# Merged delta-rule and attention stage: another order of the steps of neighbouring chunks, and five attention units in the lead-in

## The reference

```python
# DeltaNet, per chunk: A from keys and decays, a triangular solve, then the state recurrence
m = einsum(kb, kc) * decay;  a = tril(m, -1) + eye
u, w = solve(a, [v * beta, kb * exp(gcum)])
v_new = u - w @ S
o = (q * exp(g)) @ S + (q @ k.T * decay) @ v_new
S = S * exp(g_last) + (k * exp(g_last - g)).T @ v_new
# differential attention, per head and block of 128 queries, causal
amap = softmax(q1 k1) - lam * softmax(q2 k2);  out = amap @ v
```

## Time and profile before

| | |
|---|---|
| median of three runs | 1760.65 us |
| profiled execution | 1762.61 us |
| its span, first to last instruction | 1761.0 us |
| TensorE busy | 1644.0 us |
| VectorE busy | 996.0 us |
| ScalarE busy | 524.2 us |
| GpSimd busy | 290.5 us |
| merged stage | 434.8 to 730.4 us of the span |

### The profile page before, as it was taken

How to read it: one execution, slowest core, us unless ns; L and a number is a source line. 1 busy time by engine, 2 the same in 40 slices (tenths; PEclk the granted TensorE clock), 3 DMA queues, 4 the chain that set the end, 5 groups by cost and what they waited for, 6 DMA issues and landing times.

```text
span 1761.0 us, 27513 instructions
## 1 busy us (share of the span) xinstructions
PE 1644.0 (93%) x10506; PEld 1534.7 (87%) x10506; DVE 996.0 (57%) x1416; ACT 524.2 (30%) x810; POOL 290.5 (16%) x668
## 2 busy tenths in 40 slices
PE   5999999998789899788599999999999999999998
PEld 4999999897577787664399999999999999999997
DVE  4454368776467667337335565565564565555554
ACT  4344332332244344232322231122121221221214
POOL 2200012122555464233100000000000000000000
PEclk9999999999799999888699999999999999999999
DMA  4321111231112311272431221010210110111103
GB/s 143 123 60 39 45 40 37 74 98 61 51 34 55 85 27 35 72 273 72 154 84 39 73 60 59 25 60 16 67 58 14 60 60 24 60 48 36 48 0 108
DMA packets 144530, 113.34 MB, mean 64 GB/s; under 512 B 18987, under 2 KB 132157, under 8 KB 143030
## 3 DMA queue, kind: packets, MB, share of 16 engines
q1 hardware_dynamic: 138802, 100.43, 19.1%
q0 software_dynamic: 2304, 8.39, 1.3%
q10 hardware_dynamic: 3350, 3.53, 0.6%
HBM read 90.59 MB, written 21.74 MB: 64 GB/s over the span
## 4 chain that ended last, share of the span: by engine, by line
PE 48%; DVE 1%; ACT 1%; issue 0%; DMA 0%; SPq 0%; ACTq 0%; DVEq 0%
PE f_up L2905 28%; PE f_down L2912 14%; PE f_up L181 4%; PE f_up L2865 1%; PE f_up L2892 0%; PE f_up L2912 0%; PE f_up L2950 0%; DVE h_rstd L2745 0%; DMA f_rows<-in_ffn_conv_b 0%; DVE o_lo L2725 0%; PE f_up L2939 0%; PE f_down L2855 0%; ACT f_tail_tok L2673 0%; DVE w_lo L2694 0%; DVE dn_lo L2836 0%
## 5 line engine op out<-in xcount | busy, mean ns | idle before, releaser
L2905 PE MATMUL f_up<-h_hi,w_hi 128*128 128x352 f32 x1032 | 335.1, 325 | 1.9 <-DVE w_lo L2694 1.2
L2905 PE MATMUL f_up<-h_hi,w_lo 128*128 128x352 f32 x1032 | 333.4, 323 | 0.0
L2905 PE MATMUL f_up<-h_lo,w_hi 128*128 128x352 f32 x1032 | 333.4, 323 | 0.0
L181 PE MATMUL proj<-x_hi,win_hi 128*128 128x352 f32 x672 | 227.4, 338 | 5.3 <-issue 3.0
L181 PE MATMUL proj<-x_hi,win_lo 128*128 128x352 f32 x672 | 217.5, 324 | 0.0
L181 PE MATMUL proj<-x_lo,win_hi 128*128 128x352 f32 x672 | 217.3, 323 | 0.0
L2905 PEld LDWEIGHTS f_up<-h_hi,w_hi 128*128 128x128 f32 x1032 | 193.8, 188 | 2.5 <-DVE w_lo L2694 1.5
L2905 PEld LDWEIGHTS f_up<-h_hi,w_lo 128*128 128x128 f32 x1032 | 194.0, 188 | 0.0
L2905 PEld LDWEIGHTS f_up<-h_lo,w_hi 128*128 128x128 f32 x1032 | 193.8, 188 | 0.0
L2912 PE MATMUL f_down<-f_g_hi,dn_hi 128*128 128x352 f32 x512 | 165.3, 323 | 0.0
L2912 PE MATMUL f_down<-f_g_hi,dn_lo 128*128 128x352 f32 x512 | 164.7, 322 | 0.0
(11 more groups left out here) (438 smaller groups left out, 2932.4 us busy)
## 6 DMA issues: line engine op xcount, KB each, us to landing
w_raw<-in_w_up SPq DMA_DIRECT2D x44, 512.0 KB, 3.8
win_raw<-in_w_in SPq DMA_DIRECT2D x28, 512.0 KB, 4.1
dn_raw<-in_w_down SPq DMA_DIRECT2D x11, 1024.0 KB, 5.1
p_key<-in_cache_k SPq DMA_DIRECT2D x32, 256.0 KB, 3.5
feat<-in_cache_v POOLq DMA_DIRECT2D x24, 256.0 KB, 5.0
x_scratch<-feat SPq DMA_DIRECT2D x1, 4224.0 KB, 13.4
feat<-x_scratch SPq DMA_DIRECT2D x8, 528.0 KB, 8.8
feat<-in_x_prompt SPq DMA_DIRECT2D x8, 512.0 KB, 8.6
```

Source lines behind the costliest of these rows:

```text
L181: mm = nc.tensor.matmul(out, w[:, k, :], x[:, k, g * TG:(g + 1) * TG], start=(k == 0 and i == 0), stop=(k == KT - 1 and i == 2))
L2905: mm = nc.tensor.matmul(up[u % RING][:, 0:TG], a[s][:, kk, :], b, start=(kk + x == 0), stop=(kk == KT - 1 and x == 2))
```

## The change

The lead-in gets five periods with a unit each (EARLY = 5), so the plan has 37 periods. 27 units are left for the chunks; the last period of the chunks 3 to 7 has none, and chunk 7 has units in its first three. The key products and their weighting of chunk n + 2 (KK, B, so AT(n+2)) move to the last period of chunk n; KQ(n+1) goes to period 1, turn_keys(n+1) stays in period 2 but ahead of the scores, R(n+2) moves from period 3 to 2, V(n+1) stays in 3. state_w and state_next stand both in period 0, state_out in period 1, before the scores. `STEP` says in which lead-in period a step of chunk 0 or 1 stands. GpSimd does block_inverse before the first two cut_offs. The waits on the `side` bank follow the new order. The rest of the kernel is the same.

```diff
@@ -1053,14 +1053,24 @@
     v_rows = o["v_prompt"].rearrange("a b (n p) h d -> p (a b n) h d", p=P)
 
 
-    EARLY = 3
+    EARLY = 5
     plan, a = [], 0
     for n in range(-1, NC):
-        for p in range(PER):
-            free = n < 0 and p >= EARLY or n == NC - 1 and a >= NU
-            plan.append((n, p, None if free else a, plan[-1][2] if plan else None))
-            a += not free
-    assert a == NU and plan[-1][2] is None
+        for p in range(EARLY if n < 0 else PER):
+            left = NU - a
+            idle = n >= 0 and p == PER - 1 and left <= (PER - 1) * (NC - 1 - n)
+            plan.append((n, p, None if idle else a, plan[-1][2] if plan else None))
+            a += not idle
+    assert a == NU
+
+    STEP = {"keys_keys": (0, 3), "spread_beta": (0, 3), "cumulate": (None, 1), "keys_queries": (1, None), "turn_keys": (2, None),
+            "spread_decay": (None, 2), "turn_values": (3, None)}
+
+    def chunk_at(n, p, what, period, ahead):
+
+        if n < 0:
+            return STEP[what].index(p) if p in STEP[what] else None
+        return n + ahead if p == period and n + ahead < NC else None
 
     def diagonal(scratch):
 
@@ -1209,10 +1219,10 @@
                 if n + 2 < NC:
                     rows(n + 2)
                 if n + 1 < NC:
+                    block_inverse(n + 1)
                     cut_off(n + 1, 0)
-                    block_inverse(n + 1)
+                    cut_off(n + 1, 1)
                     queries(n + 1)
-                    cut_off(n + 1, 1)
                 if n + 2 < NC:
                     strengths(n + 2)
 
@@ -1235,8 +1245,6 @@
             def keys_keys(n):
                 pe.wait_ge(arg_ready, n + 1)
                 pe.wait_ge(e_row_ready, n + 1)
-                if n >= 1:
-                    pe.wait_ge(vb_ready, n)
                 for h in range(H):
                     k = feat[:, H + h, toks(n)]
                     mm = nc.tensor.matmul(side[:, h * P:(h + 1) * P], k, k, start=True, stop=True)
@@ -1248,8 +1256,11 @@
                 nc.tensor.matmul(side[:, :], c["ones"][:, :], row_b[:, :, :], start=True, stop=True).then_inc(B_done, 1)
 
             def keys_queries(n):
-                pe.wait_ge(AT_ready, n + 1)
-                if n >= 2:
+                if n == 0:
+                    pe.wait_ge(AT_ready, 1)
+                elif n == 1:
+                    pe.wait_ge(vb_ready, 1)
+                else:
                     pe.wait_ge(o_kept, n - 1)
                 for h in range(H):
                     mm = nc.tensor.matmul(side[:, h * P:(h + 1) * P], feat[:, H + h, toks(n)], feat[:, h, toks(n)], start=True, stop=True)
@@ -1263,10 +1274,10 @@
 
             def turn_values(n):
                 if n + 1 < NC:
-                    pe.wait_ge(arg_ready, n + 2)
-                    pe.wait_ge(e_row_ready, n + 2)
-                pe.wait_ge(kbg_ready, n + 1)
-                pe.wait_ge(kdec_ready, n + 1)
+                    pe.wait_ge(AT_ready, n + 2)
+                else:
+                    pe.wait_ge(kbg_ready, n + 1)
+                    pe.wait_ge(kdec_ready, n + 1)
                 for h in range(H):
                     mm = nc.tensor.transpose(side[:, h * P:(h + 1) * P], feat[:, 2 * H + h, toks(n)], c["ident"][:, :])
                 mm.then_inc(vt_done, 1)
@@ -1315,10 +1326,9 @@
 
             def state_w(n):
                 pe.wait_ge(w_kept, n + 1)
-                if n + 2 < NC:
-                    pe.wait_ge(AT_ready, n + 3)
+                if n + 1 < NC:
+                    pe.wait_ge(vb_ready, n + 2)
                 else:
-                    pe.wait_ge(vb_ready, NC)
                     pe.wait_ge(o_kept, n)
                 if n == 0:
                     pe.wait_ge(state_zero, 1)
@@ -1389,17 +1399,22 @@
                         join(n, p)
                     else:
                         solve_u(n)
-                if p == 2 and n + 2 < NC:
-                    cumulate(n + 2)
-                if p == 0 and n + 1 < NC:
-                    keys_keys(n + 1)
-                if p == 1 and n >= 1:
-                    state_next(n - 1)
-                if p == 2 and n + 1 < NC:
-                    keys_queries(n + 1)
-                if p == 3 and n + 2 < NC:
-                    spread_decay(n + 2)
-                if a is not None:
+                elif a is not None:
+                    scores(a)
+                t = chunk_at(n, p, "cumulate", 2, 2)
+                if t is not None:
+                    cumulate(t)
+                t = chunk_at(n, p, "turn_keys", 2, 1)
+                if t is not None:
+                    turn_keys(t)
+                t = chunk_at(n, p, "keys_keys", 3, 2)
+                if t is not None:
+                    keys_keys(t)
+                if n >= 1 and p == 0:
+                    state_w(n - 1)
+                if n >= 1 and p == 1:
+                    state_out(n - 1)
+                if n >= 0 and a is not None:
                     scores(a)
                 if n >= 0:
                     if p < NLV:
@@ -1408,18 +1423,22 @@
                         solve_w(n)
                 if last is not None:
                     turn_map(last, 0)
-                if p == 0 and n + 1 < NC:
-                    spread_beta(n + 1)
-                if p == 1 and n >= 1:
-                    state_out(n - 1)
-                if p == 2 and n + 1 < NC:
-                    turn_keys(n + 1)
-                if p == 3 and n + 1 < NC:
-                    turn_values(n + 1)
+                t = chunk_at(n, p, "spread_beta", 3, 2)
+                if t is not None:
+                    spread_beta(t)
                 if last is not None and groups_of(last) == 2:
                     turn_map(last, 1)
-                if p == 0 and n >= 1:
-                    state_w(n - 1)
+                t = chunk_at(n, p, "keys_queries", 1, 1)
+                if t is not None:
+                    keys_queries(t)
+                t = chunk_at(n, p, "spread_decay", 2, 2)
+                if t is not None:
+                    spread_decay(t)
+                t = chunk_at(n, p, "turn_values", 3, 1)
+                if t is not None:
+                    turn_values(t)
+                if n >= 1 and p == 0:
+                    state_next(n - 1)
                 if last is not None:
                     multiply(last)
             state_w(NC - 1)
@@ -1487,22 +1506,24 @@
                         keep_M(n, p)
                     else:
                         keep_u(n)
-                if p == 2 and n + 2 < NC:
-                    keep_gcum(n + 2)
-                if p == 3 and n + 2 < NC:
-                    decays(n + 2)
+                if n >= 1 and p == 1:
+                    keep_o(n - 1)
+                t = chunk_at(n, p, "cumulate", 2, 2)
+                if t is not None:
+                    keep_gcum(t)
                 if last is not None:
                     keep_map(last, 0)
-                if p == 3 and n >= 0:
+                if n >= 0 and p == 3:
                     keep_w(n)
                 if a is not None:
                     exps(a, 0)
-                if p == 1 and n >= 1:
-                    keep_o(n - 1)
                 if last is not None and groups_of(last) == 2:
                     keep_map(last, 1)
                 if a is not None:
                     exps(a, 1)
+                t = chunk_at(n, p, "spread_decay", 2, 2)
+                if t is not None:
+                    decays(t)
                 if last is not None:
                     keep_out(last)
             keep_o(NC - 1)
@@ -1604,27 +1625,35 @@
 
             arguments(0)
             for n, p, a, last in plan:
-                if p == 0 and n + 1 < NC:
-                    keys_decayed(n + 1)
-                if p == 1 and n >= 1:
-                    next_state(n - 1)
-                if p == 2 and n + 1 < NC:
-                    queries_decayed(n + 1)
-                if p == 3 and n + 2 < NC:
-                    arguments(n + 2)
-                if a is not None:
+                if n < 0 and a is not None:
+                    maxima(a)
+                if n >= 1 and p == 0:
+                    decayed_state(n - 1)
+                    new_values(n - 1)
+                t = chunk_at(n, p, "turn_keys", 2, 1)
+                if t is not None:
+                    keys_by_token(t)
+                t = chunk_at(n, p, "keys_keys", 3, 2)
+                if t is not None:
+                    keys_decayed(t)
+                if n >= 0 and a is not None:
                     maxima(a)
                 if n >= 0 and p < NLV:
                     extended(n, p)
-                if p == 0 and n + 1 < NC:
-                    keys_weighted(n + 1)
-                if p == 0 and n >= 1:
-                    decayed_state(n - 1)
-                    new_values(n - 1)
-                if p == 2 and n + 1 < NC:
-                    keys_by_token(n + 1)
-                if p == 3 and n + 1 < NC:
```

(15 more changed lines are left out.)

## The result

| | us |
|---|---|
| before, median of 4 | 1761.16 (1760.35 to 1762.85) |
| changed kernel, median of 4 | 1781.68 (1780.92 to 1782.67) |
| ratio, 95% interval | 1.0114 (1.0098 to 1.013) |
| forecast | 1750.2 (1744.5 to 1757.5) |
| span of the profiled execution | 1781.1, before 1761.0 |

What follows compares the result with a forecast made beforehand. TensorE, busy 1644.0 of 1761.0 us, was taken as the bound, so only its idle or low-clock time could pay. Terms: -8.7 - 5.45 - 0.1 + 3.7 = -10.5, giving 1750.2 us against the median, range 1744.5 to 1757.5.

Steps and rivals of the forecast that it cites:

- The two holes: TensorE's waits before the first joins of chunks 1 and 4, for the block inverse's round trip, would go: gain 8.7 us.
- the keys held SP: Early cache keys on SP delay chunk 4's AT store; rival: its hole stays, total 1756.7 us, chance 0.12.
- The 2 us of slack for chunk 4: DD would be loaded 2 us before chunk 4's first join needs it, so that hole is probably covered.
- The lead-in: Before chunk 0: five units make the first join 5.3 us later, chunk 0 saves 5.4; net -0.1 us.
- Short waits of TensorE: PSUM bank waits from the first join on would sum to 18.7 us against 15.0 before: cost 3.7 us.
- the two patterns: Bare second transpose groups wait 0.73 us for ScalarE; V behind B waits 0.9 us for keys_weighted.
- Moves that I cost at nothing: Reordered state steps, bank waits and GpSimd's block_inverse and cut_off would cost 0 us; 4.5 kept for the range.
- Rival 2: VectorE is late at chunk starts beside GpSimd's rows and cut_off: price 4.5 us, total 1754.7 us, chance 0.13.
- The clock: TensorE's three low-clock stretches, at 505.1, 604.1 and in the tail, would go: gain 5.45 us.
- The convoy: V waits up to 2.36 us longer on the side bank in seven last periods: total 1766.7 us, chance 0.06.

Runs made afterwards that it cites:

- e1: Changed kernel plus a GpSimd wait for VectorE's difference of period 1's unit, between block_inverse and the run of cut_off, cut_off and queries, chunks 0 to 6: 1758.7 us.
- e5: Changed kernel with only GpSimd's order put back to that of the kernel before (cut_off, block_inverse, queries, cut_off): 1763.5 us.
- e9: Like e6, but GpSimd's two rows of chunks 2 to 7 also go behind the wait for VectorE's difference: 1752.8 us.
- e11: Changed kernel with two pauses in GpSimd's run behind the inverse, each product waiting for the one before: 1769.6 us.
- e6: Like e1, with V moved behind the product of the last period's unit on TensorE: 1763.6 us.
- e2: Changed kernel with four units in the lead-in instead of five (EARLY = 4): 1759.3 us.
- e3: Changed kernel with the product in queries done twice, so GpSimd's run behind the inverse is four whole-tile products instead of three: 1788.2 us.

## Why the prediction was wrong

*The two holes* (-8.7): right. Neither join waits, and the keys held SP without harm, as I had it. The 2 us of slack for chunk 4 are seen in e1, where the long waits don't stretch the chunks ahead: DD is there 4.2 us after 598.77, and the join starts at 604.63, 1.7 later. e5 shows that they hang on the new GpSimd order. (In that sum 17.7 and 2.3 give 20.0 us for the DD load, not 20.2; nothing hangs on it.)

*The lead-in* (first join 5.3 us later): right in size in this trace. It takes 43.85 us instead of 39.39, 4.5 more. In e9 and e11, with five units too, it took 40.8 and 40.6 at a higher clock, so the size is in part luck.

*Short waits of TensorE* (18.7 in sum from the first join): the two patterns are there with the sizes of rows 9, 0.73 between bare groups and 0.85 before V. But TensorE's idle time behind the first join is 38.2 us (48.4 less 10.3). Of the 19.5 too little, 15.3 are the waits for the difference in the chunks (18.1 less 2.8 in the lead-in) and 1.6 one wait of solve_u behind a held difference; the other 2.6 are spread. In e1, which takes the run away, the idle time there is 24.1.

*Moves that I cost at nothing*: here is the step that failed. "On GpSimd only block_inverse and cut_off change places" gave the wrong picture of time. (It isn't the whole of the program either: the second cut_off also goes ahead of queries, so that three products follow the inverse instead of two.) I computed that the inverse would end 17.7 us into the chunk and used that for DD alone. What stands behind the inverse on GpSimd's queue moves with it. The trace has the first product 17.2 us into chunk 1 and the scaling of the large unit of period 1 18.0 us into it, with its map due at once. Had I laid the three products behind my 17.7 us beside VectorE's operations, they would have met it. The cost that I put at nothing is 15.3 us of waits and the clock behind them. I knew the hold from rows 11 (1.86 instead of 0.29) and looked for it only at the chunk's start.

*Rival 2* named the right pair of engines, at the wrong place and too cheap: 1.5 us a chunk, by the length of one product. A run without pauses holds until its end: 2.7 to 4.0 us beyond the operation's own time. e6 and e9 show that the place I did name is real as well, but it decides only after V's wait is gone. The Trainium skill, SBUF — State Buffer, section SBUF: two separate sides, has the lock and says that the one that comes second is blocked for the whole instruction. The trace goes further: the hold outlasts the instruction, 3.39 us beside a run of 3.70 in three instructions, and 4.32 where the scaling had started 0.07 us ahead of them.

*The clock* (-5.45): wrong by its condition "if no new low stretch comes". The four long waits brought four, two smaller delays two more. The term came out as +8.0 instead. In e1, where the waits are gone, so are those four.

Together: 19.5 of idle time and 13.5 of clock, less 0.8 in the lead-in, are 32 us, and the forecast missed by 31. Both parts have one cause in the main, and e1, e2, e3, e5 and e11 move it five ways. The sum without it was still 8.5 us too good: e1 takes 1758.7 for a forecast of 1750.2. 5.4 of that is idle time beyond the 18.7, small waits for ScalarE and VectorE in chunks 0, 6 and 7 among it, and two low stretches, at 484.1 and 688.9, are most of the rest. *The convoy* (rival 4) did not come: V waits 0.85 each time.

## What to carry to other kernels

When an engine's long step starts earlier, everything queued behind it starts earlier too: write down where each of those instructions lands, and beside what it lands on the other engines, before calling the move free. On a pair of engines that hold each other up, look for runs of whole-tile operations, not for single ones, and put a wait ahead of them, or pauses between them, so that the latency-bound engine goes first. Where one wait of 3 us is followed by a stretch of TensorE at its lower clock, as four were here, it costs nearly twice its length: 12.1 us of waits, and half of the 20.9 us of work in the four stretches.

## What the runs showed of the hardware that I had not expected

- VectorE's scaling from SBUF to SBUF doesn't get in between two GpSimd products that follow each other without a wait: 3.39 and 4.32 us for 0.69 and 0.75 us of work, ending 0.5 to 0.6 us behind the run in each case. Size doesn't help: a product of one column, 0.15 us alone, took 4.25 us in e2. A product that waits for the one ahead (0.17 us idle in the timeline) lets it in: at most 1.89 us in e11.
- The combining step, which reads two tiles of SBUF, is held in the same way (4.64 and 4.52 us in chunks 4 and 6). keys_by_token, with one input in PSUM, wasn't: 0.68 us at 530 in e1, while GpSimd's run was going on.
- It goes both ways: in e11 the third product took 2.23 us instead of 1.25 while VectorE was at its combining step.
